# Causal scores without the early queries' late keys, the norm's division moved behind level 0, and one filler of two steps: a change to a block of RWKV-7, windowed attention and convolutional FFN

## The chip, the cores and the metric

The kernel runs on one core of a Trainium2 chip. Its engines work side by side, each through its own queue, and meet at semaphores: TensorE (PE in the rows; PEld are its weight loads), VectorE (DVE), ScalarE (ACT), GpSimd (POOL) and SyncE (SP). The metric is the device time of one execution in microseconds; smaller is better.

## What is computed

One layer over 512 tokens of width 1024: a norm, one wide projection, two branches (an RWKV-7 recurrence over 16 heads of 64 and windowed attention with a sink), a gated sum with projections, and a gated FFN with a convolution. The change touches only the recurrence:

```python
def step(S, inp):
    r_t, w_t, k_t, v_t, aa_t, bb_t = inp
    sa = jnp.einsum('bhvk,bhk->bhv', S, aa_t)
    S = S * w_t[:, :, None, :] + sa[..., None] * bb_t[:, :, None, :] + v_t[..., None] * k_t[:, :, None, :]
    y_t = jnp.einsum('bhvk,bhk->bhv', S, r_t)
    return S, y_t

_, y = lax.scan(step, S0, (tm(rh), tm(wh), tm(kh), tm(vh), tm(-kk), tm(kk * ah)))
mean = jnp.mean(y, axis=-1, keepdims=True)
var = jnp.mean(jnp.square(y - mean), axis=-1, keepdims=True)
y = (y - mean) * lax.rsqrt(var + GN_EPS)
```

## The kernel before

The recurrence is computed in chunks of 128 tokens, four per head (NT = 4, C = 128), for two heads at a time, which lie in partitions 0 to 63 and 64 to 127. There are eight such pairs, n = 0 to 7. For each chunk the kernel forms scores between all keys s of the chunk (partitions of the result) and all queries t (columns): `bp` and `kp` are the two kinds of keys, `ar` holds two kinds of queries side by side, 128 columns each. Only s < t (or s <= t) counts, so DVE copies the scores from PSUM through the mask `causal` into `gb` and `gk`, whose other entries stay zero (`masked`, L1515 to L1527: a tiny memset and a `copy_predicated`, eight per pair, f = 0 to 7). The part of gb for the first kind of query is inverted by doubling, in seven levels (`invert`). From Y and X of one level come those of the next: TensorE multiplies, DVE masks and adds, ACT copies.

Each engine's order is written out by hand; there is no planner. Around the change it is this, for a pair n with the pair before it, d = n - 1:

TensorE, `scores` (L2242): 8 matmuls for bp and 8 for kp, each of 256 columns, into the banks `SCORE_BANK`; the scores of the last two masks reuse banks 0 and 1 and wait for `g_ready` 2. A 32-bit matmul stands as two records in the trace, so each kind has 16. Then the variance of the pair before (`norm_var`, L2227, with the bonus sums), a filler step `fill("scores")`, the row of deviations turned (`turned_var`, L2238), the values `z` turned (waits for mask 3), `bp` turned (mask 4), the spread reciprocals `ysq` of the pair before turned (`deviations`, L2211, waits for `vex_ready`), a filler step `fill("centred")`, and `kp` turned (mask 8). `turned` (L2193) is four transposes. Then `invert` (L2277): it waits for `n1_ready`, takes a filler step, does level 0 (its second half waits for the value tokens, `vp_ready`), two filler steps, and from level 1 on: the half products as soon as Y is there (`y_ready`, at level 1 `y_start`), a filler step, the update, which waits for v1 and X.

A filler step is three matmuls of 512 columns of a projection of the rest of the layer (L2038 to L2040). The tables `SLOT_A` to `SLOT_C` and `FILL_FIRST`, `FILL_LAST` (L2442 on) say how many go where. Their total is fixed.

DVE (L1713 on): the last steps of the scan of pair d, which make bp and kp; the low part of a weight tile (`weights`, L1351); in n = 1 and 2 the token shift of a tile (`fill_low`, L1384); six masks; `deviations(d)` (L1510: reciprocal of the turned deviations, then a spread copy into ysq); two masks; `value_tokens` (L1485); then `invert`, which begins with the product `xx` (L1574, of n1 and `first_level`, both 16 bit in SBUF) and the masks of level 0 (L1589).

ACT: the squares and the scaled copy of y (L1030, L1031), `deviation` (L1037, L1038), then `score_copy` (L1067), which waits for mask 4 and copies gb into the 16-bit `n1`, then a weight tile and the token copies.

POOL: `bonus_product` (L737), `odd_columns` (L744), then `remainder` (L730), n2 = gb - n1, as soon as n1 is there, then the DMAs of the bonus and of the key norms and a product (L842). Ahead of the first pair it clears gb (`cleared` 1, L789), and after the first pair's bp and kp are made it clears gk (`cleared` 2, L821) and zp (`cleared` 3).

The waits of `masked` before:

```python
if n == 0:
    dve.wait_ge(cleared, 1 + f // 4)
dve.wait_ge(g_ps, n * 8 + f + 1)
```

## Time and profile before

| | us |
|---|---|
| median of 3 runs | 1024.65 |
| lowest, highest | 1024.53, 1024.91 |
| the profiled execution | 1024.74 |
| its span, first to last instruction | 1023.0 |
| TensorE busy | 1011.2 (99%) |
| DVE busy | 736.7 (72%) |
| ACT busy | 517.3 (51%) |
| POOL busy | 224.4 (22%) |
| mean granted TensorE clock | 0.999 |

The rows below are of one profiled execution. Times count from its first instruction. A row of a timeline gives the start, the length, the engine, the line of the kernel, the operation, the tiles written and read, their shapes and the number of records merged; in brackets stands idle time of the engine before it and what ended it. Consecutive operations of an engine overlap a little, as each is recorded with its whole latency: what one costs in a row of its kind is the distance between starts.

### The profile page before, as it was taken

How to read it: one execution, taken by the hardware profiler on the slowest of the kernel's cores; microseconds unless marked ns; L12 is line 12 of the kernel's file. 1: busy time of each engine (PE TensorE's matmuls, PEld its weight loads, DVE VectorE, ACT ScalarE, POOL GpSimd, SP SyncE). 2: the span in 40 equal slices, each digit the busy share in tenths (PEclk: the TensorE clock that was granted, in tenths of full speed). 3: DMA queues.
4: the chain of work that ended last, by engine and by line, in shares of the span. 5: the costliest groups of instructions: out<-in, count | busy, mean ns of one | idle time of the engine just before them, and what ended most of it. 6: DMA issues, size and time to landing. Idle time of an engine off the chain costs nothing.

```text
span 1023.0 us, 18730 instructions
## 1 busy us (share of the span) xinstructions
PE 1011.2 (99%) x7098; PEld 805.8 (79%) x7098; DVE 736.7 (72%) x1233; ACT 517.3 (51%) x869; POOL 224.4 (22%) x298
## 2 busy tenths in 40 slices
PE   8999999999999999999999999999999999999997
PEld 7888888777777777777777888888888888888886
DVE  5224666788988888888877565367777777789786
ACT  6435766844445445345453322265455444467744
POOL 8541356230321412314220554000000000000000
PEclk9999999999999999999999999999999999999999
DMA  7874465331303313214355867613333333336662
GB/s 201 240 223 135 130 218 197 91 78 42 87 24 74 87 63 86 57 62 119 95 163 151 239 232 257 202 36 103 88 103 89 97 101 103 90 116 223 206 186 116
DMA packets 161292, 133.25 MB, mean 130 GB/s; under 512 B 32730, under 2 KB 137736, under 8 KB 161224
## 3 DMA queue, kind: packets, MB, share of 16 engines
q1 hardware_dynamic: 147552, 88.37, 29.9%
q0 software_dynamic: 13520, 43.90, 13.9%
q8 instruction: 47, 0.77, 0.3%
q14 instruction: 22, 0.17, 0.1%
q10 hardware_dynamic: 151, 0.04, 0.0%
HBM read 111.83 MB, written 20.45 MB: 129 GB/s over the span
## 4 chain that ended last, share of the span: by engine, by line
PE 94%; DVE 2%; ACT 1%; issue 1%; DMA 1%; POOL 0%; ACTq 0%; DVEq 0%; POOLq 0%
PE ps L2082 15%; PE ps L2085 14%; PE ps L2084 14%; PE ps L2038 6%; PE ps L2040 5%; PE ps L2039 5%; PE ps L2640 3%; PE ps L2642 3%; PE ps L2641 3%; PE ps L2254 3%; PE ps L2388 2%; PE ps L2195 2%; PE ps L2576 1%; PE ps L2574 1%; PE ps L2575 1%; PE ps L2337 1%
## 5 line engine op out<-in xcount | busy, mean ns | idle before, releaser
L1351 DVE TENSOR_TENSOR wlo<-raw,whi 128x1024 fp32r<-128x1024 f32 x106 | 140.4, 1325 | 128.4 <-ACT whi L885 110.5
L885 ACT ACTIVATE whi<-raw 128x1024 fp32r<-128x1024 f32 x116 | 122.8, 1059 | 129.6 <-PE ps L2085 117.6
L2082 PE MATMUL ps<-xnh,whi 128*128 128x512 f32 x336 | 130.7, 389 | 0.0
L2084 PE MATMUL ps<-xnl,whi 128*128 128x512 f32 x336 | 130.7, 389 | 0.0
L2085 PE MATMUL ps<-xnh,wlo 128*128 128x512 f32 x336 | 130.7, 389 | 0.0
L2082 PE MATMUL ps<-xh,whi 128*128 128x512 f32 x232 | 91.5, 394 | 1.0 <-DVE xl L1369 1.0
L2084 PE MATMUL ps<-xl,whi 128*128 128x512 f32 x232 | 90.4, 390 | 0.0
L2085 PE MATMUL ps<-xh,wlo 128*128 128x512 f32 x232 | 90.3, 389 | 0.0
L2038 PE MATMUL ps<-xh,whi 128*128 128x512 f32 x192 | 89.5, 466 | 0.0
L2040 PE MATMUL ps<-xh,wlo 128*128 128x512 f32 x192 | 76.1, 396 | 0.0
L2039 PE MATMUL ps<-xl,whi 128*128 128x512 f32 x192 | 75.3, 392 | 0.0
L2085 PEld LDWEIGHTS ps<-xnh,wlo 128*128 128x128 f32 x336 | 63.1, 188 | 13.2
L2084 PEld LDWEIGHTS ps<-xnl,whi 128*128 128x128 f32 x336 | 63.1, 188 | 13.1
L2082 PEld LDWEIGHTS ps<-xnh,whi 128*128 128x128 f32 x336 | 63.1, 188 | 13.0
L1087 ACT ACTIVATE xx<-ps 128x256 f16<-128x256 f32 x96 | 32.2, 383 | 69.0 <-PE ps L2294 68.2
L2082 PEld LDWEIGHTS ps<-xh,whi 128*128 128x128 f32 x232 | 43.5, 188 | 11.8 <-DVE wlo L1351 1.2
L2085 PEld LDWEIGHTS ps<-xh,wlo 128*128 128x128 f32 x232 | 43.6, 188 | 9.0
L2084 PEld LDWEIGHTS ps<-xl,whi 128*128 128x128 f32 x232 | 43.6, 188 | 8.7
L1871 DVE TENSOR_TENSOR sq<-ps,rs 128x512 f32<-128x512 f32 x44 | 30.4, 691 | 23.4 <-PE ps L2085 18.4
L737 POOL TENSOR_TENSOR z<-z,kmod 128x512 f32<-128x512 f32 x8 | 16.2, 2023 | 126.4 <-DVE kp L1480 126.4
L2040 PEld LDWEIGHTS ps<-xh,wlo 128*128 128x128 f32 x192 | 36.0, 188 | 8.3
L1600 DVE TENSOR_TENSOR yy<-ps,yy 128x256 f16<-128x256 f32 x96 | 36.2, 419 | 8.6 <-PE ps L2337 8.1
(425 smaller groups left out, 2441.0 us busy)
## 6 DMA issues: line engine op xcount, KB each, us to landing
raw<-in_w_in SPq DMA_DIRECT2D x108, 256.0 KB, 3.2
raw<-in_w_up SPq DMA_DIRECT2D x88, 256.0 KB, 3.0
wrow<-in_w_down POOLq DMA_DIRECT2D x22, 512.0 KB, 4.7
raw<-weight_scratch SPq DMA_DIRECT2D x44, 256.0 KB, 3.4
raw<-in_w_down SPq DMA_DIRECT2D x32, 256.0 KB, 2.9
weight_scratch<-wrow POOLq DMA_DIRECT2D x11, 512.0 KB, 3.4
gates_scratch<-gst POOLq DMA_DIRECT2D x16, 256.0 KB, 3.3
raw<-in_w_proj_b SPq DMA_DIRECT2D x16, 256.0 KB, 4.1
```

The source lines that it names most:

```text
L885: act.activation(flat(whi[:, hb]), flat(raw[:, b]), ACT.Copy).then_inc(w_hi, 1)
L1087: act.activation(dst, src, ACT.Copy).then_inc(x_ready, 1)
L1351: dve.tensor_tensor(flat(lo[:, hb]), flat(raw[:, b]), flat(hi[:, hb]).bitcast(F32), ALU.subtract).then_inc(w_lo, 1)
L1600: dve.tensor_tensor(yg, low_half(ps[2 * g][:, :], lv), yg, ALU.add)\
L2038: pe.matmul(o, whi[:, hb, k, :], self.hi(k), start=k == 0, stop=False)
L2039: pe.matmul(o, whi[:, hb, k, :], self.lo(k), start=False, stop=False)
L2040: ins = pe.matmul(o, wlo[:, hb, k, :], self.hi(k), start=False, stop=k == KT - 1)
L2082: pe.matmul(ps[bank][:, :], whi[:, hb, k, :], hi(k), start=first and k == 0, stop=False)
L2084: pe.matmul(ps[bank][:, :], whi[:, hb, k, :], lo(k), start=False, stop=False)
L2085: ins = pe.matmul(ps[bank][:, :], wlo[:, hb, k, :], hi(k), start=False, stop=last and k == kn - 1)
L2254: ins = pe.matmul(ps[SCORE_BANK[f + h]][:, (j - j0) * 2 * C: (j - j0 + 1) * 2 * C], src[hs, j * C:(j + 1) * C], ar[hs, 1 - n % 2, j, :], s ...
L2640: pe.matmul(o, h_hi, hi[:, cols], start=start, stop=False)
```

## The change

Scores: the chunk's 128 queries are parted in early (0 to 63) and late (64 to 127). Early queries are multiplied with the early 64 keys only, as 64x64 pieces: head h gives the rows of the array, an even or odd chunk (e) the upper or lower half of the result's partitions in banks 2 and 3. Late queries are multiplied with all 128 keys, into banks 0 and 1 (bp) and 4 and 5 (kp). DVE masks the early scores first, four operations on 64 partitions, each for bp and kp together, then the late scores of bp (two), then the value tokens, then the late scores of kp (two). gb and gk become the halves of one tensor gg. ACT's copy n1 waits for six masks instead of four. In the first pair the early masks wait for `cleared` 2.

The norm: DVE's `deviations(d)` moves from between the sixth and seventh mask to after the masks of level 0; TensorE's transposes of its result move to level 1, ahead of `fill((1, "masks"))`. `turned_var` moves behind the turning of bp.

Filler: `fill("scores")` goes, and "centred" has two steps instead of one (three instead of two in the first pair).

```diff
--- before.py
+++ after.py
@@ -52,7 +52,8 @@
 RKV_TILES = 17
 RKV_LOOP = RKV_TILES - 1
 FILL_BANK = (7, 4, 7)
-SCORE_BANK = (0, 1, 2, 3, 4, 5, 0, 1)
+EARLY_BANK = (2, 3)
+LATE_BANK = ((0, 1), (4, 5))
 WARM = 24
 HALF_EXP = float(-0.5 * np.exp(-0.5))
 NEG = -1e30
@@ -272,11 +273,12 @@
         brow = take("brow", [P, P])
         lih = take("lih", [P, T], F32R)
         take = taker(KVR, PREP)
-        gb = take("gb", [P, NT, 2, 2 * C])
+        gg = take("gg", [P, NT, 2, 2, 2, C])
+        gb, gk = (gg[:, 2 * i:2 * i + 2].rearrange("p x e h q t -> p (x e) h (q t)")
+                  for i in range(2))
         gst = take("gst", [P, 2, T])
         xx = take("xx", [P, NT, 2, C], F16)
         ysb = take("ysb", [P, T])
-        gk = take("gk", [P, NT, 2, 2 * C])
         rkcols = take("rkcols", [P, P // NT])
 
 
@@ -1063,7 +1065,7 @@
                 act.activation(flat(ktok), ps[1][:, :], ACT.Copy).then_inc(tok_ready, 1)
 
             def score_copy(n):
-                act.wait_ge(g_ready, n * 8 + 4)
+                act.wait_ge(g_ready, n * 8 + 6)
                 act.activation(n1[:, :, :, :], gb[:, :, :, 0:C], ACT.Copy).then_inc(n1_ready, 1)
 
             def hi_part(dst, src, i):
@@ -1512,19 +1514,40 @@
                 chain(dve.reciprocal(by_token(ystd[:, :]), by_token(ps[6][:, P:2 * P])))
                 spread(ysq, ystd).then_inc(vex_ready, 1)
 
-            def masked(n, f):
-
-                j0, h = (f % 4) // 2 * 2, f % 2
-                dst = (gb, gk)[f // 4][:, j0:j0 + 2, h, :]
+            def two_parts(t, ts):
+                return t.rearrange("p (q t) -> p q t", q=2)[:, :, ts]
+
+            def predicated(dst, mask, scores, f):
+                dve.memset(carrier[:, f:f + 1], 0.0)
+                dve.copy_predicated(dst, mask.bitcast(U32).unsqueeze(1)
+                                    .to_broadcast([mask.shape[0], NT, 2, C // 2]), scores)\
+                    .then_inc(g_ready, 1)
+
+            def late_masked(n, i, h):
+                f = 4 + 2 * i + h
                 if n == 0:
-                    dve.wait_ge(cleared, 1 + f // 4)
+                    dve.wait_ge(cleared, 1 + i)
                 dve.wait_ge(g_ps, n * 8 + f + 1)
-
-                dve.memset(carrier[:, f:f + 1], 0.0)
-                dve.copy_predicated(dst, causal[:, :].bitcast(U32).unsqueeze(1)
-                                    .to_broadcast([P, 2, 2 * C]),
-                                    ps[SCORE_BANK[f]][:, :].rearrange("p (j t) -> p j t", j=2))\
-                    .then_inc(g_ready, 1)
+                predicated((gb, gk)[i][:, :, h, :].rearrange("p j (q t) -> p j q t", q=2)
+                           [:, :, :, C // 2:], two_parts(causal[:, :], slice(C // 2, C)),
+                           ps[LATE_BANK[i][h]][:, :].rearrange("p (j q t) -> p j q t", j=NT, q=2), f)
+
+            def early_masked(n, h, e):
+                if n == 0:
+                    dve.wait_ge(cleared, 2)
+                dve.wait_ge(g_ps, n * 8 + 4)
+                predicated(gg[0:HD, :, e, h, :, 0:C // 2],
+                           two_parts(causal[0:HD, :], slice(0, C // 2)),
+                           ps[EARLY_BANK[h]][e * HD:(e + 1) * HD, :]
+                           .rearrange("p (x q t) -> p x q t", x=NT, q=2), 2 * h + e)
+
+            def masked(n, i):
+                if i == 0:
+                    for h in range(2):
+                        for e in range(2):
+                            early_masked(n, h, e)
+                for h in range(2):
+                    late_masked(n, i, h)
 
             def add_bonus(d):
                 dve.wait_ge(bonus_ps, 1)
@@ -1588,6 +1611,8 @@
                                    for t in (vg, ps[2 * g][:, :])]
                         dve.tensor_tensor(by_unit[0], by_unit[1], mask, ALU.mult)\
                             .then_inc(v_ready if lv else y_start, 1)
+                    if lv == 0 and d is not None:
+                        deviations(d)
                     if lv == 6:
                         fill_low(3 * n)
                     if lv in (4, 5):
@@ -1706,9 +1731,9 @@
                 piece()
             attention_copy(7)
             weights(n + 2)
-            for f in range(8):
-                masked(0, f)
+            masked(0, 0)
             value_tokens(0)
+            masked(0, 1)
             invert(0, None, True)
             for n in range(1, PAIRS):
                 key, rates, factor, modified, removed, a_tilde, r_tilde, b_hat, k_hat = prepare(n)
@@ -1717,12 +1742,9 @@
                              (2, "s"): [r_tilde], (3, "z"): [b_hat], (3, "u"): [k_hat]})
                 weights(N_FILL + 3 * n)
                 fill_low(3 * n - 1)
-                for f in range(6):
-                    masked(n, f)
-                deviations(n - 1)
-                for f in range(6, 8):
-                    masked(n, f)
+                masked(n, 0)
                 value_tokens(n)
+                masked(n, 1)
                 invert(n, n - 1, n < PAIRS - 1)
 
             def gated_bonus(d):
@@ -2244,32 +2266,46 @@
                 pe.wait_ge(ops_ready, n + 1)
                 if n == 0:
                     pe.wait_ge(ps_free, N_FILL - 1)
-                for f in range(0, 8, 2):
-                    src, j0 = (bp, kp)[f // 4], f % 4
-                    if f == 6:
-                        pe.wait_ge(g_ready, n * 8 + 2)
-                    for j in range(j0, j0 + 2):
-                        for h in range(2):
-                            hs = slice(h * HD, (h + 1) * HD)
-                            ins = pe.matmul(ps[SCORE_BANK[f + h]][:, (j - j0) * 2 * C:
-                                                                  (j - j0 + 1) * 2 * C],
-                                            src[hs, j * C:(j + 1) * C], ar[hs, 1 - n % 2, j, :],
+                rows = [slice(h * HD, (h + 1) * HD) for h in range(2)]
+
+                def both(hs, j, ts):
+                    return ar[hs, 1 - n % 2, j, :].rearrange("p (q t) -> p q t", q=2)[:, :, ts]
+
+                def late(i):
+                    src = (bp, kp)[i]
+                    for j in range(NT):
+                        for h, hs in enumerate(rows):
+                            ins = pe.matmul(ps[LATE_BANK[i][h]][:, j * C:(j + 1) * C]
+                                            .rearrange("p (q t) -> p q t", q=2),
+                                            src[hs, j * C:(j + 1) * C], both(hs, j, slice(HD, C)),
                                             start=True, stop=True)
-                            if j > j0:
+                            if j == NT - 1:
                                 ins.then_inc(g_ps, 1)
+
+                for i, src in enumerate((bp, kp)):
+                    for jj in range(2):
+                        o = (2 * i + jj) * C
+                        for e in range(2):
+                            j = 2 * jj + e
+                            for h, hs in enumerate(rows):
+                                ins = pe.matmul(ps[EARLY_BANK[h]][e * HD:(e + 1) * HD, o:o + C]
+                                                .rearrange("p (q t) -> p q t", q=2),
+                                                src[hs, j * C:j * C + HD], both(hs, j, slice(0, HD)),
+                                                start=True, stop=True)
+                                if i and jj:
+                                    ins.then_inc(g_ps, 1)
+                late(0)
+                late(1)
                 if d is not None:
                     norm_var(d)
-                fill("scores")
-                if d is not None:
-                    turned_var(d)
-                pe.wait_ge(g_ready, n * 8 + 3)
+                pe.wait_ge(g_ready, n * 8 + 2)
                 turned(2, z[:, n + 16, :]).then_inc(tok_ps, 1)
                 pe.wait_ge(g_ready, n * 8 + 4)
                 turned(3, bp).then_inc(tok_ps, 1)
                 if d is not None:
-                    deviations(d)
+                    turned_var(d)
                 fill("centred")
-                pe.wait_ge(g_ready, n * 8 + 8)
+                pe.wait_ge(g_ready, n * 8 + 6)
                 turned(1, kp).then_inc(tok_ps, 1)
 
             halves = [slice(h * HD, (h + 1) * HD) for h in range(2)]
@@ -2322,6 +2358,8 @@
                             if lv == 2 and g == 0:
                                 pe.wait_ge(tok_ready, n * 2 + 2)
                             transposed(g, lv - 1).then_inc(x_ps, 1)
+                    if lv == 1 and d is not None:
+                        deviations(d)
                     fill((lv, "masks"))
                     if lv == 0:
                         continue
@@ -2439,14 +2477,14 @@
                     else:
                         output(j, "u")
 
-            SLOT_A = {"scores": 1, "centred": 1, "tokens": 1, (0, "masks"): 2, (1, "masks"): 1,
+            SLOT_A = {"centred": 2, "tokens": 1, (0, "masks"): 2, (1, "masks"): 1,
                       (1, "update"): 1, (2, "masks"): 1}
             SLOT_C = {(2, "update"): 1, (3, "masks"): 1, (4, "masks"): 1, (4, "update"): 1,
                       (5, "masks"): 2, (5, "update"): 1, (6, "masks"): 1}
             SLOT_B = {"remainder": 2, "inverse": 2, (1, "state"): 1, (2, "state"): 1,
                       (3, "state"): 1, "output": 1}
             FILL = {**SLOT_A, **SLOT_C, **SLOT_B}
-            FILL_FIRST = {**FILL, "centred": 2, (3, "update"): 1}
+            FILL_FIRST = {**FILL, "centred": 3, (3, "update"): 1}
             FILL_LAST = {"tokens": 1, (0, "masks"): 2, (1, "masks"): 1, (1, "update"): 1,
                          (2, "masks"): 1, (2, "update"): 1, (3, "masks"): 1, (4, "masks"): 2,
                          (4, "update"): 1, (5, "masks"): 1, (5, "update"): 1, (6, "masks"): 1,
```

## Rows read from the trace of the kernel before

**Rows 1.** the page's first part: busy time and share of the span by engine

```profile
PE 1011.2 (99%) x7098; PEld 805.8 (79%) x7098; DVE 736.7 (72%) x1233; ACT 517.3 (51%) x869; POOL 224.4 (22%) x298
```

**Rows 2.** timeline of TensorE, fifth pair (n=4): start, length, line, tiles, shapes, count

```profile
377.05 2.00 PE L2254 MATMUL ps<-ar,bp 64*128 64x256 f32 x16
...
380.71 0.42 PE L2189 MATMUL ps<-ysq,meancols 128*32 128x128 f32 x8
380.95 0.40 PE L2189 MATMUL ps<-z,rkcols 128*32 128x128 f32 x8
381.28 0.50 PE L2038 MATMUL ps<-xh,whi 128*128 128x512 f32 x1
...
382.21 0.60 PE L2195 MATMUL ps<-ident,z 128*128 128x128 f32 x4
...
383.13 0.66 PE L2195 MATMUL ps<-ident,ysq 128*128 128x128 f32 x4
383.55 0.48 PE L2038 MATMUL ps<-xh,whi 128*128 128x512 f32 x1
...
384.46 0.66 PE L2195 MATMUL ps<-ident,kp 128*128 128x128 f32 x4
...
385.66 0.62 PE L2318 MATMUL ps<-ident,n 128*128 128x64 f16 x8
386.09 0.48 PE L2038 MATMUL ps<-xh,whi 128*128 128x512 f32 x1
...
387.57 0.42 PE L2314 MATMUL ps<-yy,n 128*128 128x64 f16 x8
387.82 0.47 PE L2038 MATMUL ps<-xh,whi 128*128 128x512 f32 x1
...
388.60 0.41 PE L2337 MATMUL ps<-v,xx 128*128 128x64 f16 x8
```

**Rows 3.** timeline of DVE over the same stretch

```profile
378.22 0.73 DVE L1524 COPY_PREDICATED gb<-causal,ps 128x512 f32<-128x512 uint32 x1 [0.29 <-issue]
...
381.40 0.73 DVE L1524 COPY_PREDICATED gk<-causal,ps 128x512 f32<-128x512 uint32 x1
...
382.41 0.21 DVE L1512 RECIPROCAL ystd<-ps 128x8 f32<-128x8 f32 x1 [0.27 <-PE ps L2240]
382.65 0.43 DVE L1499 COPY ysq<-ystd 128x512 f32<-128x512 f32 x1
383.00 0.75 DVE L1524 COPY_PREDICATED gk<-causal,ps 128x512 f32<-128x512 uint32 x1
...
385.61 0.69 DVE L1574 TENSOR_TENSOR xx<-n,first_level 128x1024 f16<-128x1024 f16 x1
386.21 0.78 DVE L1589 TENSOR_TENSOR yy<-ps,level_mask 128x256 f16<-128x256 f32 x2
```

**Rows 4.** timeline of TensorE, attention scores of one chunk and what follows

```profile
112.79 1.16 PE L2139 MATMUL ps<-kb,qc 64*128 64x128 f32 x16
113.89 0.50 PE L2082 MATMUL ps<-xh,whi 128*128 128x512 f32 x1
```

**Rows 5.** timelines of ACT and POOL, fifth pair

```profile
381.84 1.06 ACT L1067 ACTIVATE n<-gb 128x1024 f16<-128x1024 f32 x1
...
382.99 2.14 POOL L730 TENSOR_TENSOR n<-gb,n 128x1024 f16<-128x1024 f32 x1 [2.61 <-ACT n L1067]
```

**Rows 6.** first pair (n=0), TensorE, DVE, POOL; last, L1574: min/median/max in ns

```profile
219.35 0.60 PE L2195 MATMUL ps<-ident,z 128*128 128x128 f32 x4
...
216.08 0.73 DVE L1524 COPY_PREDICATED gb<-causal,ps 128x512 f32<-128x512 uint32 x1
...
216.10 1.88 POOL L821 MEMSET gk<- 128x2048 f32 x1
...
221.26 2.15 POOL L730 TENSOR_TENSOR n<-gb,n 128x1024 f16<-128x1024 f32 x1
...
L1574 DVE TENSOR_TENSOR xx<-n,first_level x8: 684/686/1481, 222.5 to 507.4; 128x1024 f16<-128x1024 f16 x8
```

## The prediction, made before the changed kernel was run

> **What bounds the kernel now.** I read the page first, then the timelines of TensorE, DVE, ACT and POOL over one pass of the loop over head pairs, then over the first pass, which differs. TensorE is busy for 99% of the span [rows 1], and over the pair loop it is fed from one hand-written queue, so the question is what that queue loses or gains per pair and whether a wait opens in it. [rows 2] is the stage concerned, in the fifth pair (n=4): scores from 377.05, the norm's variance at 380.71, a filler step at 381.28, the turned tiles, a filler step, kp turned at 384.46, a filler step, level 0 at 385.66, two filler steps, level 1 at 387.57, one filler step, the level's update at 388.60. Nowhere between these rows does TensorE stand still for more than 0.1 us. Pairs n=3 to 7 repeat this within 0.05 us. In n=1 and 2 DVE has one more evacuation ahead of the masks, in n=0 the previous pair's norm is missing. DVE is next [rows 3]: eight masks 0.63 us apart, with 0.97 us for the norm's division between the sixth and the seventh, the value tokens, the product xx at 385.61, the masks of level 0 until 386.99. It is some 0.6 us ahead of level 1. I carry one number per pair: the time of the update row, 388.60.
>
> **Scores on TensorE.** Before: 377.05 to 380.71, 3.66 us. The change keeps 16 matmuls with all 128 keys but on 128 instead of 256 columns, and adds 16 of 64x64 on 128 columns. The first kind stands in the trace: the attention scores, 8 matmuls (16 records) of the same form, take 1.10 us to the next record [rows 4], of which 8 x 0.11 is streaming and 0.2 is entering and leaving the form. Sixteen take 1.10 + 0.90 = 2.0. The second kind does not appear. Bounds: two array parts at once, as the scores do now, gives 16 x 0.11 = 1.76; four at once, as the variance does with four parts of 32 columns (8 records of 128 columns in 380.95 - 380.71 = 0.24 [rows 2]), gives 8 x 0.11 = 0.88. I take the second, because the four matmuls of a group go to four different quadrants, one after the other, just as the four of L2189 go to four column parts. Leaving for the other form adds about 0.15, by the 0.1 on either side of [rows 4]. Sum 0.88 + 0.15 + 2.0 = 3.03 us. It saves **0.63** (more in n=0, 1 and 2, where kp's second half also had to wait for banks 0 and 1). The Trainium skill ("TensorEngine Tiling (Array Packing)", Available Configurations) lists 64x64 as four tiles; no run here shows it yet.
>
> **Filler and order.** With one filler step gone from ahead of the turning, TensorE goes on: variance until 380.08 + 0.57 = 380.65 (380.71 to 381.28 before), v and bp turned and the deviations' row, 9 transposes of 0.11 (four are 383.55 - 383.13 = 0.42), until 381.64. Two filler steps take 1.48 (386.09 to 387.57), kp 0.42, one filler step 0.78: level 0 at 384.32, against 385.66. Of these 1.34 us, 0.63 are the scores, some 0.2 a form switch and two short waits, and the rest is the norm's four transposes, which return at level 1. Does anything wait on DVE? DVE still makes eight masks over 512 elements each, four of them on 64 partitions. Their duration is not in the trace; nearest are the 0.73 us of the same operation on 128 partitions with the same 512 elements [rows 3]. I take that, between 0.70 and 0.85. The first waits for the last early pass: 377.05 + 0.05 + 7 x 0.11 + 0.27 = 378.14, so DVE starts at 378.2, as before (378.22). The fourth ends at 380.82, and bp is wanted at 381.1; fine. Level 0 then takes 0.43 and two filler steps 1.48: level 1 at 386.23.
>
> **n1 and what follows from it.** This is the step that decides. ACT's copy n1 now waits for the sixth mask instead of the fourth: 378.20 + 5 x 0.63 + 0.73 = 382.08, copy until 383.18 (it takes 1.06), and POOL's subtraction n2 starts 0.09 later, at 383.27. It takes 2.14 and ends at **385.41**; before it ran from 382.99 to 385.13 [rows 5]. On DVE xx moves the other way. The division (0.97) is no longer ahead of it, so it is wanted at 385.61 - 0.97 - 0.02 = **384.62**, in the middle of n2. Before, it came 0.5 us after n2's end. What such a meeting costs stands in the first pair: of the eight xx one took 1.48 us instead of 0.69, that of the first pair, which began at 222.5, and there n2 ran from 221.26 to 223.41; xx ended 0.57 after it [rows 6]. So xx ends at 385.41 + 0.57 = 385.98 instead of 385.31. The masks of level 0 follow (0.78, starting 0.07 before that end): 386.69. Now comes the division that was moved: reciprocal and spread take 0.24 + 0.43, less 0.07: 387.29. TensorE needs it for the norm's transposes, which stand ahead of the filler step: 387.35, four transposes 0.42: 387.77, filler 0.78: update at **388.55**, against 388.60. A gain of 0.05 us. TensorE stands idle about 0.7 us at level 1 in its place, with three waits in a row (two halves of y, then the spread), and queued behind them are the filler step and the update, so nothing covers it. In n=1 and 2 DVE comes from L1384 to its first mask, later than the scores would let it, before and after; I take no gain there.
>
> The Trainium skill ("SBUF — State Buffer", section on SBUF's two separate sides) has the rule that speaks against this change: VectorE with two SBUF inputs and a GpSimd instruction that reads SBUF lock each other out of a shared port for the whole instruction. The 1.48 us of the first pair agree with it. By that rule the pairs gain 0.05 each; without it they would gain 0.7.
>
> **The first pair.** The early masks write keys of both gb and gk, so the first of them waits for `cleared` 2, POOL's memset of gk, 216.10 to 217.98; before, the first four masks ran from 216.08, beside it [rows 6]. DVE now starts at 218.02. Two masks done at 219.38, v turned from 219.44 (before 219.35, with a filler step of 0.79 already behind it), four done at 220.64, bp turned from 220.70 instead of 219.88. Then three filler steps in place of two. Against before: 0.09 later at v, 0.82 waiting at bp, 0.79 for the filler step that stood ahead and now comes after: 1.70. The masks of level 0 add to it: n1 starts after 218.02 + 5 x 0.63 + 0.75 = 221.92 and ends near 223.0, n2 from 223.1 to 225.3, xx until 225.8, masks until 226.55, some 0.1 behind level 1. Together **+1.8 us**, once. Its bounds: 0 if POOL had cleared gk by then, 2.0 with slower masks. POOL's other work, the bonus row and the key norms, starts 0.3 later in each pair; the reader of its last product, L1541, comes only at level 4. The moves of gb, gk, gst and xx within SBUF I cost at nothing: same sizes, no operation more.
>
> **Sum.** 7 pairs: 5 x -0.05 = -0.25; first pair +1.8; together +1.55. The profiled execution took 1024.74 us (span 1023.0), the median is 1024.65, so both give **1026.2 us**, +0.15%. About 0.2% (2.05 us) is what a measurement here can tell from no change. By terms the forecast has its own range of 1024.9 to 1027.6: the first pair between 1.2 and 2.0, each of seven pairs between -0.15 and +0.13.
>
> **Rivals.** *The collision costs nothing* (xx not held, or n2 over by then). Then xx ends at 385.31, the masks at 386.02, the spread at 386.62; TensorE ends level 1 at 386.23 + 0.25 = 386.48, waits till 386.68, and updates at 387.88: 0.72 saved in each of 7 pairs, 5.0, less 1.8: **1021.4**. For it: seven of eight xx ran undisturbed at 0.69 [rows 6]. Against it: these started after n2 had ended, and the one that did not took 1.48. xx comes 2.5 us after the sixth mask, n2 ends 3.3 after it, and no start of the stage shifts one against the other.
> *Two quadrants at once* (slower side). Early scores take 1.76, the first mask starts 0.88 later, and as the chain mask, n1, n2, xx, spread decides from the first mask on, all of it arrives: +0.83 in five pairs, some 0.55 in two, and 1.8 once: **1031.8**. It decides from the point where the early quadrants take more than 0.1 us above my 0.93. For it: the scores' own form runs two at a time. Against it: the four column parts of L2189.
> *Slower early masks*, at 0.75 apart instead of 0.63: n1 and n2 0.48 later in each pair, the spread too: 7 x 0.44 + 0.4 + 1.8 = 5.3, **1030.0**. Against it: patterns with short runs at level 0 and 1 cost DVE no more than long ones, 256 elements in 0.42 [rows 3].
> *The first pair does not lose*: if its masks found gk cleared, **1024.4**. Against it stands the memset's row.
>
> **Chances.** Forecast 0.62 (0.42 within 0.2%, 0.20 above, since 1026.7 is only 0.5 away). No collision cost 0.17 (faster). Two quadrants 0.08, slower masks 0.05 (both slower). First pair without loss 0.05 (same). Something of the order that I missed 0.03 (faster or same). Faster 0.19, same 0.48, slower 0.33. The range takes in the forecast's and the first rival: 1021.2 to 1028.0; the last 2 in 10 are the two slow rivals and the far ends.
>
> **What the profile after would show.** Scores of 3.0 us up to L2189; early groups of eight records 0.22 apart. xx at L1574 with 1.3 to 1.5 us in every pair, ending 0.57 after n2; if it shows 0.69, the first rival holds. TensorE's weight loads waiting for the spread ysq at level 1. In the first pair DVE's first mask at POOL's memset end, and TensorE idle for 1.9 and 0.8 us around v and bp. Wrong would be: level 0 not over 1.2 us earlier than before in n=3 to 7, an update earlier by over 0.2, or a first pair that loses under 1.

## The result, and the profile after

The changed kernel takes **1032.39 us** (median of 6 runs, 1031.82 to 1032.69) against 1024.88 us for the kernel before beside it (6 runs, 1024.53 to 1025.06): ratio **1.0072**, 95% interval 1.0061 to 1.0083. It is slower by 7.5 us. The forecast was 1026.2 with a range up to 1028.0, so the time lies outside it. The profiled execution took 1032.26 us, its span is 1030.5.

The page's first part, with [rows 1] as its counterpart, and from its fourth part the shares of the chain of work that ended last:

```profile
PE 1010.2 (98%) x7354; PEld 806.7 (78%) x7354; DVE 745.2 (72%) x1233; ACT 516.2 (50%) x869; POOL 223.9 (22%) x298
...
PE 85%; DVE 9%; issue 3%; ACT 1%; DMA 1%; POOL 0%; ACTq 0%; DVEq 0%; POOLq 0%
```

TensorE is busy for a microsecond less, and the span is 7.5 us longer: the time went into standing still, and the chain now runs through DVE for 9% of the span (2% before, by the same line of that page). The timeline of TensorE in the fifth pair (n=4) shows where, to be laid beside [rows 2]:

```profile
382.21 0.67 PE L2291 MATMUL ps<-ar,bp 64*64 64x128 f32 x16
382.70 0.62 PE L2291 MATMUL ps<-ar,kp 64*64 64x128 f32 x16
383.25 1.16 PE L2278 MATMUL ps<-ar,bp 64*128 64x128 f32 x16
...
385.23 0.43 PE L2211 MATMUL ps<-ysq,meancols 128*32 128x128 f32 x8
...
388.59 0.60 PE L2217 MATMUL ps<-ident,kp 128*128 128x128 f32 x4
...
389.93 0.62 PE L2354 MATMUL ps<-ident,n 128*128 128x64 f16 x8
...
392.33 0.62 PE L2350 MATMUL ps<-yy,n 128*128 128x64 f16 x8 [0.33 <-DVE yy L1612]
393.13 0.65 PE L2217 MATMUL ps<-ident,ysq 128*128 128x128 f32 x4 [0.18 <-DVE ysq L1501]
...
394.33 0.41 PE L2375 MATMUL ps<-v,xx 128*128 128x64 f16 x8
```

The scores take 385.23 - 382.21 = 3.02 us, forecast 3.03. The early quadrants, 32 records in 1.04 us (0.93 forecast), run four at once. But the update, L2375, stands 12.12 us after the first score, and before it was 388.60 - 377.05 = 11.55. Ahead of it, at level 1, are the two waits that were foreseen, for y and for the spread. DVE, ACT and POOL over the same stretch answer to [rows 3] and [rows 5]:

```profile
383.47 0.73 DVE L1522 COPY_PREDICATED gg<-causal,ps 64x512 f32<-64x512 uint32 x1 [0.38 <-issue]
...
384.24 0.74 DVE L1522 COPY_PREDICATED gg<-causal,ps 64x512 f32<-64x512 uint32 x1
...
385.01 0.75 DVE L1522 COPY_PREDICATED gg<-causal,ps 64x512 f32<-64x512 uint32 x1
...
385.80 0.74 DVE L1522 COPY_PREDICATED gg<-causal,ps 64x512 f32<-64x512 uint32 x1
386.48 0.06 DVE L1521 MEMSET carrier<- 128x1 f32 x1
386.57 1.39 DVE L1522 COPY_PREDICATED gg<-causal,ps 128x512 f32<-128x512 uint32 x2
...
390.46 1.37 DVE L1597 TENSOR_TENSOR xx<-n,first_level 128x1024 f16<-128x1024 f16 x1
```

```profile
388.00 1.06 ACT L1069 ACTIVATE n<-gg 128x1024 f16<-128x1024 f32 x1 [1.52 <-DVE gg L1522]
```

```profile
389.14 2.15 POOL L732 TENSOR_TENSOR n<-gg,n 128x1024 f16<-128x1024 f32 x1 [3.59 <-ACT n L1069]
```

Two things are to be seen. xx takes 1.37 us and ends 0.54 after n2 (391.29), in every pair (eight times 1.35 to 1.39): the collision came as forecast. And the early masks start **0.77 us apart**, not 0.63, though each is recorded with the same 0.73 as before; the next one starts only after its neighbour has ended. The sixth mask ends 5.75 us after the first score, and ACT's n1, which waits for it, starts at 5.79.

The first pair, TensorE's timeline, and then windows (columns: stretch, its length, busy time and instructions of PE, PEld, DVE, ACT, POOL, granted clock, DMA share, GB/s):

```profile
219.53 0.66 PE L2217 MATMUL ps<-ident,z 128*128 128x128 f32 x4 [1.99 <-DVE gg L1522]
221.05 1.12 PE L2217 MATMUL ps<-ident,bp 128*128 128x128 f32 x4 [0.87 <-DVE gg L1522]
221.82 0.78 PE L2060 MATMUL ps<-xh,whi 128*128 128x512 f32 x1
222.39 0.63 PE L2061 MATMUL ps<-xl,whi 128*128 128x512 f32 x1
```

```profile
219.50:221.80 2.30, 1.40 (x8) 1.17 (x9) 2.22 (x7) 0.00 (x0) 1.70 (x4) 0.84 0.24 30
221.80:224.50 2.70, 2.70 (x8) 2.16 (x7) 2.67 (x7) 1.06 (x1) 0.94 (x1) 0.50 0.69 82
```

The 1.99 and 0.87 us of idleness were forecast as 1.9 and 0.8. What was not: right behind them the granted clock falls to 0.50, the 1.2 GHz level. It is 0.50 in the whole second window, and 0.84 in the first, which is 0.74 us of 2.30 at half; together that is 3.4 us, and the filler matmuls in it follow each other after 0.43 us instead of 0.23.

| update after the pair's first score | before | after | forecast change | measured change |
|---|---|---|---|---|
| n=0 | 11.23 | 14.79 | +1.8 | +3.56 |
| n=1, 2 | 11.82 | 12.30 | 0 each | +0.48 each |
| n=3 to 7 | 11.52 to 11.55 | 12.11 to 12.12 | -0.05 each | +0.58 each |
| sum | | | +1.55 | +7.4 |

The sum accounts for the difference of 7.5 but for 0.1; no other stage is needed.

### The profile page after: what moved, and what is told of

It is laid out like the page before. It is cut to its first block, busy times and chain, and to the rows that moved or that the text cites. A ratio compares the mean times of both kernels' runs of the same rounds, so it can differ in the third digit from the quotient of the medians.

```text
span 1030.5 us, 19242 instructions
## 1 busy us (share of the span) xinstructions
PE 1010.2 (98%) x7354; PEld 806.7 (78%) x7354; DVE 745.2 (72%) x1233; ACT 516.2 (50%) x869; POOL 223.9 (22%) x298
## 4 chain that ended last, share of the span: by engine, by line
PE 85%; DVE 9%; issue 3%; ACT 1%; DMA 1%; POOL 0%; ACTq 0%; DVEq 0%; POOLq 0%
PE ps L2104 14%; PE ps L2107 14%; PE ps L2106 14%; PE ps L2060 5%; PE ps L2062 4%; PE ps L2061 4%; PE ps L2678 3%; PE ps L2680 3%; PE ps L2679 3%; DVE gg L1522 2%; PE ps L2613 1%; PE ps L2614 1%; PE ps L2612 1%; PE ps L2375 1%; PE ps L2330 1%
## 5 line engine op out<-in xcount | busy, mean ns | idle before, releaser
L2107 PEld LDWEIGHTS ps<-xh,wlo 128*128 128x128 f32 x232 | 43.6, 188 | 9.1
L1522 DVE COPY_PREDICATED gg<-causal,ps 64x512 f32<-64x512 uint32 (+1 forms) x64 | 45.7, 739 | 4.9 <-issue 1.9
```

The lines of the kernel that those rows point to most:

```text
L1522: dve.copy_predicated(dst, mask.bitcast(U32).unsqueeze(1) .to_broadcast([mask.shape[0], NT, 2, C // 2]), scores)\
L2107: ins = pe.matmul(ps[bank][:, :], wlo[:, hb, k, :], hi(k), start=False, stop=last and k == kn - 1)
```

## The experiments

Times written "at 12.12" count from the first score of the pair. Edits are against the changed kernel unless said otherwise; "before" in brackets is the kernel before, run beside that experiment. Three variants ran only once: late_half, which masks the late scores with the wrong half of the mask; no_shift, which leaves out the odd blocks' early scores; and all_wide, which takes them from the even blocks. Each stands for what its trace shows; its time is one value without an interval.

### Each part alone

**division_only** is the kernel before with nothing but the division behind level 0 and the filler of two steps; the scores and their eight masks are the old ones.

```diff
-                for f in range(6):
-                    masked(n, f)
-                deviations(n - 1)
-                for f in range(6, 8):
-                    masked(n, f)
+                for f in range(8):
+                    masked(n, f)
...
+                    if lv == 0 and d is not None:
+                        deviations(d)
...
```

> The kernel before, with only the norm's division behind level 0 (and TensorE's transposes of it at level 1) and the one filler of two steps; scores, masks and the wait for four masks as they were. Theory (moving the division is free as long as n1 comes after four masks: n2 ends at 8.1 us after the scores' start, xx is wanted at 7.5 and ends at 8.7, the spread at 10.0, just when TensorE wants it): update 0.3 earlier than before in each pair, 1024.9 - 2.1 = 1022.8 us, with xx at about 1.1 us. Rival (the division behind level 0 costs by itself): 1024.9 or more.

Measured: **1022.15 us** (1022.07 to 1022.68; before 1025.01), ratio 0.9973, interval 0.9963 to 0.9983. This part is a gain, and the kernel is faster than both. xx meets n2's end and takes 1.03 us here, but nobody sees it: level 1 starts at 9.75 with no wait, and the update is at 11.18.

**early_only** is the changed kernel with division, value tokens and fillers put back where they were; only the scores, the masks and n1's wait for six masks are new.

```diff
                 masked(n, 0)
-                value_tokens(n)
+                deviations(n - 1)
                 masked(n, 1)
+                value_tokens(n)
...
```

> The changed kernel with the division back between the sixth mask and the last two, value tokens behind the eighth, and the filler steps and transposes as in the kernel before; only the early and late scores and their masks are new. Theory (the masks on 64 partitions cost 0.14 each and n1 waits for two more of them; without the moved division n2 has ended when xx comes): xx 0.69 us in pairs n>=1, update 0.3 to 0.4 later than before, and the first pair 2 us later: 1024.9 + 2.5 + 2.2 = 1029.6 us. Rival (the early scores pay on TensorE when nothing else is moved): under 1025 us.

Measured: **1027.94 us** (1027.73 to 1029.20), ratio 1.0030, interval 1.0020 to 1.0041. The early masks are 0.77 apart, xx takes 0.79, the update is at 11.66. That is 0.1 later than before, not 0.3 to 0.4 as expected; the first pair, at 13.57 instead of 11.23, is most of the loss. The 0.63 us that the scores save is lost again at TensorE's wait for the spread, which the slower masks push back:

```profile
386.16 0.66 PE L2216 MATMUL ps<-ident,ysq 128*128 128x128 f32 x4 [0.78 <-DVE ysq L1501]
```

So the parts alone give -2.9 and +2.9 against the kernel before beside them (1025.01), and together +7.5: they interfere.

### Why the early masks are 0.77 us apart

**carrier64** clears the column ahead of an early mask on 64 partitions only.

```diff
-                dve.memset(carrier[:, f:f + 1], 0.0)
+                dve.memset(carrier[0:mask.shape[0], f:f + 1], 0.0)
```

> The changed kernel, with the tiny memset ahead of each early mask on 64 partitions, as many as the mask has, instead of 128. Theory A (what parts the early masks by 0.77 us instead of 0.63 is the change of width between the memset and the copies): the starts of the early masks are 0.63 apart again, the sixth mask, n1, n2, xx and the spread come 0.4 to 0.57 earlier in each pair, 1028 to 1029 us. Rival B (a copy on 64 partitions, or one that moves data between partitions, is slow to hand over by itself): still 0.77 apart, 1032.4 us.

Measured: still 0.77, 1032.20 us (1030.78 to 1032.45). The theory fell.

**wide_even** widens the masks of the even blocks to all 128 partitions.

```diff
-                predicated(gg[0:HD, :, e, h, :, 0:C // 2],
+                w = HD if e else P
+                predicated(gg[0:w, :, e, h, :, 0:C // 2],
...
```

> The changed kernel, but the early masks of even chunks (e = 0) work on 128 partitions instead of 64; the mask is zero in the other 64, so nothing more is written. Those of odd chunks stay at 64. Theory (the operation after a copy on 64 partitions starts 0.14 us late, whatever the memset is): after an even one the next starts 0.63 us later, after an odd one 0.77; 0.28 per pair, 1032.4 - 2.1 = 1030.3 us. Rival (the distance comes from the access pattern or from the banks the early scores lie in): 0.77 everywhere, 1032.4 us.

Measured: 0.76 to 0.78 throughout, 1032.40 us (1031.05 to 1032.53). Width by itself isn't it.

**late_half** gives the late masks the early masks' half of the causal mask.

```diff
-                           [:, :, :, C // 2:], two_parts(causal[:, :], slice(C // 2, C)),
+                           [:, :, :, C // 2:], two_parts(causal[:, :], slice(0, C // 2)),
```

> Only the slice of the causal mask that the four late masks read is changed: columns 0 to 63 of each half, as the early masks read, instead of 64 to 127 (so the late scores are masked wrongly; all shapes and addresses of source and destination stay). Theory M: that slice, with its many zeros, is what makes an early mask hold back the next instruction, 0.77 us instead of 0.65. Then all eight masks are 0.77 apart, the last two as well, and the time is about 1033. Theory D: it is the destination, whose blocks of the early masks lie 4 KB apart (every second query block) and those of the late ones 2 KB. Then the early masks stay at 0.77, the late ones at 0.65, and the time at 1032.4.

Measured: late masks 0.65, early 0.77, as they were: theory M fell. The one time, 1030.69 us, is below both expectations; in its first pair the clock didn't fall (below).

**by_source** puts the scores of bp and kp, not of even and odd blocks, on the two halves of a bank; TensorE's loop over the early scores, left out here, follows.

```diff
-                predicated(gg[0:HD, :, e, h, :, 0:C // 2],
+                predicated((gb, gk)[e][0:HD, :, h, :].rearrange("p j (q t) -> p j q t", q=2)
+                           [:, :, :, 0:C // 2],
...
```

> The four quadrants are given out another way: the upper and lower output half of a bank are now the scores of bp and of kp, and no longer the even and the odd blocks. Each early mask then writes only gb or only gk, in blocks 2 KB apart as the late masks do, and from the same number of scores. Matmuls, waits and counts stay. Theory D (destination): masks 0.64 apart throughout, the sixth ends 0.5 us earlier, and n1, n2, xx, the spread and the update with it: 0.48 in each of seven pairs, 3.4 us, so 1032.4 becomes 1029.0 (1028.4 to 1029.7), update at 11.65 after the first score. Theory M, or any cause in the mask or in the 64 partitions: still 0.77 apart, and 1032.4 (1031.8 to 1032.9).

Measured: 0.77, update at 12.09, 1031.09 us (1030.73 to 1032.05). Theory D fell as well.

**no_shift** and **no_carrier** take away the move between partitions, and the memset with its wait.

```diff
-                predicated(gg[0:HD, :, e, h, :, 0:C // 2],
-                           two_parts(causal[0:HD, :], slice(0, C // 2)),
+                es = slice(e * HD, (e + 1) * HD)
+                predicated(gg[es, :, e, h, :, 0:C // 2],
+                           two_parts(causal[es, :], slice(0, C // 2)),
```

> The second of each two early masks, which reads output partitions 64 to 127 of a bank and writes partitions 0 to 63, now writes partitions 64 to 127 (source, mask and destination unshifted; the odd blocks' early scores are thereby left out). Theory S: it is the move between partitions that keeps an instruction from starting in the tail of its neighbour, 0.77 instead of 0.63 us; as every early mask and the fifth stand beside a moving one, all five are slowed. Then all masks are 0.63 to 0.65 apart, the update comes 0.5 us earlier, and the time is 3.4 us less, about 1029. Theory C (the column of memset between the masks, whose wait has long been met when it comes to its turn): still 0.77, and 1032.4 or, without the fall of the clock in the first pair, 1030.7.

```diff
-                dve.memset(carrier[:, f:f + 1], 0.0)
+                if f not in (1, 2, 3):
+                    dve.memset(carrier[:, f:f + 1], 0.0)
...
-                if n == 0:
+                if n == h == e == 0:
                     dve.wait_ge(cleared, 2)
-                dve.wait_ge(g_ps, n * 8 + 4)
+                if h == e == 0:
+                    dve.wait_ge(g_ps, n * 8 + 4)
```

> The memsets of one column ahead of the second, third and fourth early mask, and these masks' waits, are left out: all four early quadrants are announced at once, so the first mask's wait stands for all. Theory C: these memsets run only after the mask before them has ended, since nothing is left for them to wait for in its shadow, and each costs 0.06 plus the hand-over; then the early masks come 0.63 apart (the fifth, which keeps its memset, still 0.77), the sixth mask ends 0.4 us earlier, and the time is 7 x 0.4 = 2.8 us less: 1029.6 (1029.0 to 1030.2). Theory S (the move between partitions): about 0.70 to 0.77 apart, and 1031 to 1032.7.

Measured: no_carrier 0.77 apart without any memset between them, 1030.84 us (1030.70 to 1032.27): theory C fell. In no_shift theory S fell too: it went the wrong way, 1033.63 us (one run), and gave the clue. Its DVE timeline:

```profile
384.84 0.74 DVE L1522 COPY_PREDICATED gg<-causal,ps 64x512 f32<-64x512 uint32 x1
385.64 0.06 DVE L1521 MEMSET carrier<- 128x1 f32 x1
385.72 0.74 DVE L1522 COPY_PREDICATED gg<-causal,ps 64x512 f32<-64x512 uint32 x1
386.40 0.06 DVE L1521 MEMSET carrier<- 128x1 f32 x1
386.49 0.73 DVE L1522 COPY_PREDICATED gg<-causal,ps 64x512 f32<-64x512 uint32 x1
```

Behind a mask that writes partitions 64 to 127 (384.84) the next comes after 0.88 us, behind one that writes 0 to 63 (385.72) after 0.77. In the first case the memset between them, which writes from partition 0 again, starts only at 385.64, 0.06 after the mask ended, and the mask behind it later still. So the partition at which an instruction starts costs something, and here two instructions in a row pay.

**all_wide** starts every mask at partition 0.

```diff
-                predicated(gg[0:HD, :, e, h, :, 0:C // 2],
-                           two_parts(causal[0:HD, :], slice(0, C // 2)),
-                           ps[EARLY_BANK[h]][e * HD:(e + 1) * HD, :]
+                predicated(gg[:, :, e, h, :, 0:C // 2],
+                           two_parts(causal[:, :], slice(0, C // 2)),
+                           ps[EARLY_BANK[h]][:, :]
```

> All four early masks read and write all 128 partitions from partition 0, so that every mask of a pair has the same set of partitions (the odd blocks' early scores are thereby taken from the even blocks'). Theory W: an instruction starts in the tail of its neighbour only where both use the same partitions; in the trial with the even masks widened each still stood beside a narrow one. Then the masks come 0.63 to 0.65 apart, the sixth ends 0.5 us earlier, n1, n2, xx and the update with it: 3.4 us less, 1029.0 (with the fall of the clock in the first pair) or 1027.4 (without). Rival, that neither number nor place of partitions matters but something else of the early scores: 0.77 apart, 1030.7 to 1032.4.

Measured, DVE's timeline:

```profile
381.54 0.74 DVE L1522 COPY_PREDICATED gg<-causal,ps 128x512 f32<-128x512 uint32 x1 [0.38 <-issue]
...
382.17 0.74 DVE L1522 COPY_PREDICATED gg<-causal,ps 128x512 f32<-128x512 uint32 x1
...
382.80 0.75 DVE L1522 COPY_PREDICATED gg<-causal,ps 128x512 f32<-128x512 uint32 x1
```

0.63 to 0.65 apart, update at 11.55 instead of 12.12, and 1028.02 us (one run) with the fall of the clock in it. With full-speed masks the fifth pair is back at the time of the kernel before, 11.55, and within 0.05 of the forecast (11.50).

**e_major** tells whether it is the width or the place: same narrow masks, other order.

```diff
-                    for h in range(2):
-                        for e in range(2):
+                    for e in range(2):
+                        for h in range(2):
                             early_masked(n, h, e)
...
-                pe.wait_ge(g_ready, n * 8 + 2)
+                pe.wait_ge(g_ready, n * 8 + 3)
                 turned(2, z[:, n + 16, :]).then_inc(tok_ps, 1)
```

> The four early masks in another order: first the two that read output partitions 0 to 63 (banks 2 and 3), then the two that read 64 to 127, and v is turned after three masks instead of two, as bank 2 is free only then. Theory Q: an instruction of VectorE starts in the tail of the one ahead only if the two read PSUM from the same starting partition; otherwise it waits for its end. In the changed kernel's order (0, 64, 0, 64, 0) four of the six masks change it, all of them 0.77 after their neighbour; here (0, 0, 64, 64, 0) two do. Then the second and the fourth mask follow after 0.63 to 0.65, the third and the fifth after 0.77, the sixth mask ends 0.26 earlier, and with it n1, n2, xx and the update: 11.86 us after the first score in the fifth pair. 7 x 0.26, and 0.26 in the first pair: 2.1 us less, 1030.3 (1029.2 to 1030.7, less 1.3 more where the clock doesn't fall in the first pair). Rival N, that a narrow mask always holds back the next: 0.77 throughout, 1032.4. The Trainium skill (VectorE: DVE Perf Modes, section Two Vector instructions with no wait between them) has a model in which an instruction is held when its input from a memory starts in another quadrant of partitions than the last one read from there; theory Q is that model, and it would give these times.

Measured, DVE's timeline in the fifth pair:

```profile
382.51 0.73 DVE L1522 COPY_PREDICATED gg<-causal,ps 64x512 f32<-64x512 uint32 x1 [0.38 <-issue]
...
383.14 0.73 DVE L1522 COPY_PREDICATED gg<-causal,ps 64x512 f32<-64x512 uint32 x1
...
383.91 1.39 DVE L1522 COPY_PREDICATED gg<-causal,ps 64x512 f32<-64x512 uint32 x2
...
385.34 1.39 DVE L1522 COPY_PREDICATED gg<-causal,ps 128x512 f32<-128x512 uint32 x2
```

Distances 0.63, 0.77, 0.66, 0.77, 0.64 (the third and the fifth lie inside the rows that merge two), and within 0.02 the same in the other pairs: exactly where the PSUM input's first partition changes it is 0.75 to 0.79, and two narrow masks from the same place follow nearly as fast as wide ones. Update at 11.84 (expected 11.86), **1030.25 us** (1028.88 to 1030.34), expected 1030.3. For masks that start at partition 0 or 64, the two places tried here, this settles it.

### The meeting of xx and n2

**xx_first** lets n2 wait until xx is done (`x_start` counts finished xx).

```diff
                 pool.wait_ge(n1_ready, n + 1)
+                pool.wait_ge(x_start, n + 1)
```

> The changed kernel with one wait more: POOL begins n2 only when DVE's product xx is done, so the two can't meet. Theory (the meeting is what holds xx back, and what follows xx decides when TensorE can go on): L1597 falls from 1.37 to 0.69 us, the update of level 1 comes 0.69 earlier in each of seven pairs, 1032.4 - 4.8 = 1027.6 us. Rival (xx is held back by something else, or another wait is just behind it): L1597 still over 1 us, or the time moves by less than 1 us, 1031.5 to 1032.4.

Measured: 1037.74 us (1037.08 to 1039.06), ratio 1.0129, interval 1.0112 to 1.0145, slower still, against 1027.6 expected; the update stands at 12.72 in the fifth pair. The timelines of DVE and POOL:

```profile
391.81 0.68 DVE L1598 TENSOR_TENSOR xx<-n,first_level 128x1024 f16<-128x1024 f16 x1
...
393.31 1.75 DVE L1502 COPY ysq<-ystd 128x512 f32<-128x512 f32 x1
```

```profile
392.64 2.13 POOL L733 TENSOR_TENSOR n<-gg,n 128x1024 f16<-128x1024 f32 x1 [5.73 <-DVE xx L1598]
```

xx is free at 0.68, and now the spread runs into n2: 1.75 us instead of 0.43, ending 0.29 after n2. So this f32 copy within SBUF is held too, though it has one input. The two products with a PSUM input between xx and the spread (L1613, 0.79 for both, to 393.19) passed at their usual length while n2 ran. The later updates account for 0.6 in each of seven pairs; where the rest was lost wasn't traced.

**n2_late** moves n2 behind the spread as well.

```diff
                 pool.wait_ge(n1_ready, n + 1)
+                pool.wait_ge(x_start, n + 1)
+                if n:
+                    pool.wait_ge(vex_ready, n)
```

> The changed kernel; POOL begins n2 only when DVE has done both xx and, from the second pair on, the spread ysq. (With the wait for xx alone n2 met the spread instead: it took 1.74 us and ended 0.28 after n2, and the update came 0.6 later.) Theory (n2 holds back whichever of the two DVE operations it meets, and the chain xx, masks, spread decides level 1): xx 0.69 and the spread 0.43 us in every pair, the update near 11.4 us after the scores' start instead of 12.1, 1032.4 - 4.9 = 1027.5 us. Rival (the late n2 runs into something further down, the inversion's end or the bonus): what is gained at level 1 is lost again, 1031 to 1033 us.

Measured: 1063.29 us (1062.97 to 1064.25), ratio 1.0375, interval 1.0357 to 1.0392. Level 1 went as forecast (update at 11.40), but POOL works in order: the bonus row's DMA, which needs nothing of n2, stood behind it. POOL's timeline:

```profile
362.40 2.13 POOL L735 TENSOR_TENSOR n<-gg,n 128x1024 f16<-128x1024 f32 x1 [7.01 <-DVE ysq L1504]
364.48 0.56 POOL L811 DMA_DIRECT2D bonus_scratch<-brow  x1
...
373.81 1.26 POOL L847 TENSOR_TENSOR z<-z 128x512 f32<-128x512 f32 x1 [4.73 <-DMA z<-bonus_scratch]
```

The last product waits for that transfer, DVE waits for the product, and TensorE for DVE (2.64 us at L2378), with the clock at half behind it again:

```profile
375.10 0.75 DVE L1567 SCALAR_TENSOR_TENSOR ysb<-ysb,par,z 128x512 f32<-128x512 f32 x1 [3.29 <-POOL z L847]
```

The fault lay in the queue, as the next run shows.

**bonus_first** puts the bonus row's transfers ahead of n2, and clears gk early (as in clear_early, below).

```diff
-                remainder(n)
                 bonus_back(n - 1)
+                remainder(n)
...
```

> n2 waits for xx to have ended its wait on TensorE and for the spread, and the bonus row's two transfers of the previous pair are put ahead of it in GpSimd's queue (they need only ACT's row, there at 4.3 us after the first score); gk is cleared ahead of the last attention transfer. Theory, that what the two parts lose together is xx meeting n2, and that the earlier trial of a late n2 lost by its queue alone: xx 0.68 us, spread until 10.15, update at 11.40 from the third pair on (12.12 in the changed kernel, 11.55 before), n2 until 12.0, GpSimd's product done by 14 instead of 23 us, no wait at L2387. Against before: 5 x -0.15, two pairs -0.1, the first +0.7 to +1.3: 1024.7 (1023.8 to 1026.2). Rival, that a late n2 costs by itself (its reader on TensorE, or another meeting with VectorE): update early but a stall after the levels, 1029 or more.

Measured: **1024.89 us** (1024.70 to 1025.30), ratio 1.0000, interval 0.9991 to 1.0010. DVE and POOL:

```profile
386.32 0.69 DVE L1601 TENSOR_TENSOR xx<-n,first_level 128x1024 f16<-128x1024 f16 x1
...
387.83 0.43 DVE L1505 COPY ysq<-ystd 128x512 f32<-128x512 f32 x1
```

```profile
388.43 2.14 POOL L735 TENSOR_TENSOR n<-gg,n 128x1024 f16<-128x1024 f32 x1 [2.43 <-DVE ysq L1505]
...
391.76 1.30 POOL L848 TENSOR_TENSOR z<-z 128x512 f32<-128x512 f32 x1
```

Both operations at their own length, update at 11.41: the meeting costs 12.12 - 11.41 = 0.71 us a pair, 5.1 us against clear_early.

### The first pair

**clear_early** clears gk ahead of the last attention transfer; **first_fill** puts one of the three filler steps back ahead of the turning.

```diff
             attention_out(6)
-            attention_out(7)
+            pool.wait_ge(o_ps, 16)
             pool.wait_ge(ops_ready, 1)
             pool.memset(gk[:, :, :, :], 0.0).then_inc(cleared, 1)
+            attention_out(7)
```

> The changed kernel, with POOL's clearing of gk ahead of its last store of the attention's output instead of behind it. Theory: in the first pair DVE's first mask starts near 2.0 us after the scores instead of 3.55, TensorE's idle times there shrink from 2.0 and 1.1 us, and the granted clock doesn't fall to 0.50 after them, so the pair gains 1.5 from the earlier start and 1.6 from the clock: 1029.3 us. Rival (the clock falls for another reason than this idle time): 1030.9 us, with the stretch at 0.50 still there.

```diff
                 if d is not None:
                     norm_var(d)
+                else:
+                    fill("scores")
...
```

> The changed kernel, and in the first pair alone one of the three filler steps ahead of the turning again, in TensorE's longest idle time. No work is added or left out. Theory (the clock falls because TensorE stands still around the turning): the filler step fills 0.8 us, and with less idle time the clock stays at 1.00, worth 1.6 more: 1030.0 us. Rival (the clock falls regardless of it): 0.8 alone, 1031.6 us, and a stretch at 0.50.

Measured: clear_early 1030.02 us (1030.01 to 1031.46), the first pair's update at 12.58 instead of 14.79, of which the fall of the clock was part. first_fill 1031.33 us (1030.98 to 1031.77), update at 13.58. In both profiles the filler matmuls of this stretch follow each other after 0.23 us, so the clock didn't fall there. Both missed what was expected (1029.3; 1030.0 or 1031.6). In first_fill the filler step itself brought nothing to the update: late_half, which lacks it and kept its clock too, has 13.59. TensorE was 0.4 us earlier at level 0 and then stood waiting for DVE:

```profile
226.82 0.61 PE L2352 MATMUL ps<-yy,n 128*128 128x64 f16 x8 [0.39 <-DVE yy L1612]
```

One of the four runs of clear_early took 1031.46 us at a mean clock of 1.000, so a spread of 1.4 us occurs for reasons other than the clock too.

### Both cures

**e_major_bonus** is bonus_first with the masks in e_major's order.

> The same order of masks in the kernel whose n2 comes behind the spread with the bonus row's transfers ahead of it and gk cleared early (1024.9). xx meets nothing there, the update stands at 11.41, and TensorE waits at level 1 for y (0.2) and for the spread (0.2). Theory Q: sixth mask 0.26 earlier, but n1, xx and the spread depend on it or follow it on VectorE, so all of it arrives: update at 11.15 to 11.2, 8 x 0.26 = 2.1 less: 1022.8 (1022.3 to 1023.6). Rival N: 1024.9. If the gain stops at TensorE's own queue instead, 0.2 in each of seven pairs: 1023.5.

Measured: **1023.56 us** (1023.00 to 1023.83), ratio 0.9987, interval 0.9977 to 0.9996. Update at 11.15 as expected, but the total fell by 1.3 instead of 2.1: in the profiles the periods (from one pair's first score to the next pair's) of pairs 0 to 5 are 0.20 to 0.27 shorter each, that of pair 6 by 0.11, while the first score of all comes 0.32 later (215.13 against 214.81), for a reason that isn't known. This is the changed kernel with its faults mended, and division_only is still 1.4 us ahead of it: the times of the two don't overlap, the intervals of their ratios just do.

## Why the prediction was wrong

**Right.** The early quadrants four at once (3.02 us for the scores, forecast 3.03); the Trainium skill ("TensorEngine Tiling (Array Packing)", Available Configurations) lists 64x64 as four tiles, and this trace agrees, 0.11 us for four records, one in each quadrant. That xx would meet n2: it ends 0.54 after it, forecast 0.57. That this would eat what the division's move gives, at 0.7 us a pair: 0.71 measured. The Trainium skill ("SBUF — State Buffer", the section on SBUF's two separate sides) has the rule: a GpSimd operation that reads SBUF and a VectorE operation with two SBUF inputs shut each other out, and so do any GpSimd operation and a VectorE operation in a 2-port mode; whichever starts second waits. The trace agrees for xx, which has two SBUF inputs. The prediction named this case alone, and by it the spread, with one input, would have passed; in xx_first it took 1.75 us instead of 0.43, and no run shows in which mode it ran. The first pair's waits, 1.99 and 0.87 us, came as forecast. So the outline held, and the rival in which the collision costs nothing didn't come.

**Wrong, the masks' distance.** The step that failed is the term "378.20 + 5 x 0.63 + 0.73 = 382.08", and with it "The fourth ends at 380.82": it priced the hand-over between 64-partition masks, which read PSUM from alternating places, by the distance of 128-partition ones, which all read from the same place. I looked for the cost in the duration, "between 0.70 and 0.85", and the duration was right (0.73); what changed was the hand-over. Of six masks four start from another PSUM partition than the last read and come 0.77 instead of 0.63 after it: with 0.1 for a later first mask the sixth ends 0.7 later than forecast (5.75 us after the first score instead of 5.03). In all_wide full-speed masks bring the update 0.54 to 0.57 forward, 4.0 us in seven pairs; for the first pair 0.56 (0.14 x 4) is an estimate, taken up below. A sign of being wrong that the prediction named came too, level 0 not over 1.2 us earlier than before: it is 0.9 earlier (7.72 after the first score against 8.61), as the turning of bp begins at 4.38, behind the fourth mask, which was forecast to end at 3.77 and ends at 4.33. In all_wide level 0 stands at 7.17, 1.4 earlier than before. The rival "slower early masks" had the mechanism's place and nearly its size, 1030.0, and got 0.05 because patterns with short runs had cost nothing in [rows 3]; that row speaks about the elements within a partition, and the change was in the partitions. The Trainium skill ("VectorE: DVE Perf Modes", Two Vector instructions with no wait between them) has a model that names this case: an instruction is held until the earlier ones have ended if its input from PSUM starts in another quadrant of partitions than the last one read there. It fits all eight mask experiments, and even the 0.88 of no_shift, where the memset and the mask behind it would both be held. It was not weighed in the prediction, and it spoke against this change as much as the rule on the port did.

**Wrong, the first pair.** The forecast took the waiting at full clock, +1.8 us. Measured is +3.56 = 1.8 + 0.56 for the masks + 1.2 for the clock, which the prediction put at nothing. The last term comes from late_half, whose first pair has the same two waits, 2.00 and 0.87, but a granted clock of 1.00 all through:

```profile
219.30:221.60 2.30, 1.35 (x9) 1.11 (x10) 2.19 (x9) 0.00 (x0) 1.74 (x4) 1.00 0.18 25
221.60:224.30 2.70, 2.70 (x15) 2.22 (x14) 2.67 (x9) 2.00 (x3) 0.86 (x1) 1.00 0.73 82
```

There the update came at 13.59 instead of 14.79, and the whole took 1030.69 instead of 1032.26. At 13.59 it is 2.36 later than before, the forecast's 1.8 and the 0.56. In all_wide, where the clock fell, fast masks bring it to 14.42, only 0.37 forward: TensorE at half clock is then the later one, and part of what DVE gains isn't seen. So the split between masks and clock in this pair is worked out, the sum is measured. The fall followed these waits in some executions and not in others: the profiled run of by_source took 1032.05 at a mean clock of 0.997, the other three 1030.73 to 1031.23 at 0.999 or more. That the waits are a condition of it shows over all eighteen profiles: eleven have 2.5 to 3.0 us of idleness around these two turnings and eight of them show the fall; in the seven with 2.0 us or less none does. What decides from execution to execution stays open.

**The sum.** 1026.2 + 4.0 + 0.56 + 1.2 = 1032.0, against 1032.4. Of the 0.4 that is left, 0.25 is the 0.05 in each of five pairs by which even all_wide's update (11.55) stands behind the forecast's (11.50); the rest isn't accounted for.

**Why the parts interfere.** With the old scores n2 ends at 8.1, and xx, though held until 8.6, is done before TensorE asks for level 1: the division's move gains 2.9. The new scores let ACT and POOL start later (six masks, not four, and each slower), so n2 ends at 9.08 (8.08 before), and with the division gone from ahead of it xx is wanted in the middle of n2 when TensorE, 0.6 us ahead by its shorter scores, is waiting. Each part alone leaves one of the two conditions unmet.

## What to carry to other kernels

When a piece of work is cut into parts on other partitions, price the hand-over and not only the duration: sort the parts on VectorE so that neighbours read PSUM from the same first partition. A GpSimd operation beside VectorE is to be placed by the gap that it fits into, with every other instruction of its queue put in order first, and a faster TensorE stage gains nothing where the chain through DVE, ACT and POOL gets longer by the same edit. Test such an edit part by part: here one half was a gain of 2.9 us.

## What the runs showed of the hardware that was not expected

- COPY_PREDICATED over 512 elements: 0.62 to 0.67 us from start to start where the PSUM input starts at the same partition as the last one, on 64 as on 128 partitions (before, all_wide, e_major); 0.75 to 0.79 where it changes between 0 and 64; 0.86 to 0.88 where the memset between the two masks starts late as well (no_shift). Its recorded length is 0.71 to 0.76 in all these cases.
- A POOL operation that reads SBUF (n2, 2.15 us) held an f16 product of two SBUF tensors (1.37 us instead of 0.69) and an f32 copy from SBUF to SBUF (1.75 instead of 0.43), but not the products with a PSUM input (0.79 for two, in xx_first).
- The granted clock fell to 0.50 for some 3.4 us behind 1.99 and 0.87 us of idleness in one execution and stayed at 1.00 behind 2.00 and 0.87 in another (late_half). The first pair's update came 1.2 us later for it.
